# One-core decoder trunk: token factors spread by stride-zero transposes, and GpSimd normalising the probabilities of layer 0's second eight heads

## What is computed

```
def _rmsnorm(x, g):
    y = xf * lax.rsqrt(jnp.mean(xf * xf, axis=-1, keepdims=True) + EPS)
    return (y * g.astype(jnp.float32)).astype(x.dtype)

def _even_mixer(h, ...):            # layer 0
    proj = h @ w_in
    out_a = _blocked_causal_attn(...)      # 8 heads, forget-gate bias: heads 0 to 7 below
    out_b = _swa_with_sinks(...)           # 8 heads, window 128: heads 8 to 15 below
    return jnp.concatenate([out_a, out_b], axis=-1) @ w_out

# within _swa_with_sinks
    logits = jnp.where(mask, logits + bias, -jnp.inf)
    p = jax.nn.softmax(jnp.concatenate([logits, sink], axis=-1), axis=-1)[..., :-1]
    out = jnp.einsum("bnhgqk,bnkhd->bnqhgd", p.astype(v.dtype), vb)
```

## Time and profile before

| | us |
|---|---|
| time, median of 3 runs | 1150.34 |
| lowest and highest | 1149.0, 1150.37 |
| the profiled execution, its own time | 1150.78 |
| its span, first to last instruction | 1149.0 |
| PE busy in the span | 1114.7 |
| DVE, ACT, POOL busy | 878.7, 615.2, 388.0 |
| mean granted TensorE clock | 0.995 of 2.4 GHz |

### The profile page before, as it was taken

One profiled execution on the slowest core, in us unless ns is written; L12 is line 12 of the kernel. 1 busy time (PEld: TensorE's weight loads), 2 busy tenths in 40 slices (PEclk: granted clock), 3 DMA queues, 4 the chain that ended last, 5 costly groups with the idle time before them and its releaser, 6 DMA issues.

```text
span 1149.0 us, 16553 instructions
## 1 busy us (share of the span) xinstructions
PE 1114.7 (97%) x6033; PEld 944.6 (82%) x6037; DVE 878.7 (76%) x1485; ACT 615.2 (54%) x1094; POOL 388.0 (34%) x313
## 2 busy tenths in 40 slices
PE   7999999999999999999999999999999999999996
PEld 5788887888989989989967778888888888888885
DVE  6867787779668668768869999656778687787686
ACT  6777686554344354354475387854464443443443
POOL 2433433541140141151084365435521321311400
PEclk9999999999999999999999989999999999999999
DMA  5233341541522431431222000215322414315212
GB/s 167 76 115 100 103 121 42 165 129 47 174 74 72 148 89 57 146 91 55 83 74 65 28 2 27 65 38 160 116 73 92 146 56 152 99 41 183 73 37 91
DMA packets 142226, 105.55 MB, mean 92 GB/s; under 512 B 9078, under 2 KB 122017, under 8 KB 142162
## 3 DMA queue, kind: packets, MB, share of 16 engines
q1 hardware_dynamic: 140892, 104.61, 29.6%
q10 hardware_dynamic: 1270, 0.13, 0.1%
HBM read 102.56 MB, written 6.35 MB: 95 GB/s over the span
## 4 chain that ended last, share of the span: by engine, by line
PE 80%; DVE 11%; ACT 5%; issue 2%; DMA 1%; SPq 0%; ACTq 0%; DVEq 0%
PE bank L817 25%; PE bank L819 24%; PE bank L818 24%; ACT probs L1610 2%; DVE score L2552 2%; DVE probT_l L2076 1%; DVE best L2548 1%; PE bank L1027 1%; PE bank L1037 1%; PE bank L1038 1%; PE bank L1025 1%; DVE bank L2425 1%; DMA score<-in_x 1%; ACT wh L1359 1%; ACT ur L1359 1%
## 5 line engine op out<-in xcount | busy, mean ns | idle before, releaser
L1882 POOL TENSOR_TENSOR wl<-raw,wh 128x512 fp32r<-128x512 f32 x212 | 288.3, 1383 | 573.8 <-ACT wh L1359 549.9
L817 PE MATMUL bank<-ur,wh 128*128 128x512 f32 (+1 forms) x624 | 238.0, 381 | 0.2
L819 PE MATMUL bank<-ur,wl 128*128 128x512 f32 (+1 forms) x624 | 236.2, 378 | 0.0
L818 PE MATMUL bank<-ur,wh 128*128 128x512 f32 x560 | 218.0, 389 | 0.0
L1359 ACT ACTIVATE wh<-raw 128x1024 fp32r<-128x1024 f32 x107 | 111.9, 1053 | 120.4 <-PE bank L819 115.2
L817 PEld LDWEIGHTS bank<-ur,wh 128*128 128x128 f32 x624 | 117.4, 188 | 23.7 <-issue 2.5
L819 PEld LDWEIGHTS bank<-ur,wl 128*128 128x128 f32 x624 | 117.4, 188 | 21.9
L817 PE MATMUL bank<-ur 128*128 128x256 f32 (+3 forms) x352 | 119.0, 338 | 6.6 <-ACT probs L1610 2.6
L818 PE MATMUL bank<-xhl,wh 128*128 128x512 f32 (+1 forms) x336 | 124.2, 370 | 0.0
L818 PEld LDWEIGHTS bank<-ur,wh 128*128 128x128 f32 x560 | 105.2, 188 | 21.8 <-issue 0.5
L2258 DVE TENSOR_TENSOR xT<-bank,xT 128x512 f32<-128x512 f32 x112 | 74.5, 687 | 51.2 <-PE bank L819 51.1
(11 more groups left out here) (308 smaller groups left out, 2549.4 us busy)
## 6 DMA issues: line engine op xcount, KB each, us to landing
raw<-in_w_mlp SPq DMA_DIRECT2D x64, 512.0 KB, 4.0
raw<-in_w_in_e SPq DMA_DIRECT2D x18, 512.0 KB, 3.8
probs<-in_w_mlp SPq DMA_DIRECT2D x16, 512.0 KB, 4.4
rstd_qk<-in_w_mlp SPq DMA_DIRECT2D x16, 512.0 KB, 3.8
sq<-in_w_mlp SPq DMA_DIRECT2D x16, 512.0 KB, 4.8
raw<-in_w_in_o SPq DMA_DIRECT2D x10, 512.0 KB, 3.7
raw<-in_w_out_e SPq DMA_DIRECT2D x8, 512.0 KB, 3.8
score<-in_w_mlp SPq DMA_DIRECT2D x8, 512.0 KB, 6.2
```

Source lines behind the costliest of these rows:

```text
L817: mm(dst, lhs[0], rhs[0], start=start, stop=False, skip_group_check=not check)
L818: mm(dst, lhs[0], rhs[1], start=False, stop=False, skip_group_check=not check)
L819: return mm(dst, lhs[1], rhs[0], start=False, stop=stop, skip_group_check=not check)
L1882: return nc.gpsimd.tensor_tensor(dst, a, b, ALU.subtract)
```

## The change

It has two parts.

First, `diagonal` is gone. `spread` no longer multiplies ones by a diagonal matrix; it transposes, four times, a view of one column of `fin[:, 3, :]` that repeats it 128 times with stride zero. The semaphore that the diagonals raised (diag_ready) is replaced by factors_ready, which the last operation of `refined_root` raises.

Second, for heads 10 to 15 GpSimd runs `normalise`. VectorE's `sums(s + 1)` moves to the start of step s (9 to 14); its low halves of head s stand ahead of the maxima of head s+2. GpSimd's `normalise(s + 1)` stands at the head of its step s, and the spare slabs' splits no longer wait for probs_ready. Heads 8 and 9 are still normalised by VectorE.

```diff
             def spread(norm):
-                pe.wait_ge(diag_ready, NORMS.index(norm) + 1)
-                mm(bank[0][:, :], ones[:, :], sq[:, 0, :], start=True, stop=True).then_inc(spread_done, 1)
+                pe.wait_ge(factors_ready, NORMS.index(norm) + 1)
+                for a in range(NQ):
+                    last = nc.tensor.transpose(bank[0][:, P * a:P * (a + 1)], fin[:, 3, a:a + 1].to_broadcast([P, P]),
+                                               ident[:, :])
+                last.then_inc(spread_done, 1)
...
+            def normalise(j):
+                pool.wait_ge(rsum_ready, j + 1)
+                for blk, _, _, w, pc in units(j):
+                    pr = probs[:, j % 2, pc:pc + w]
+                    nc.gpsimd.tensor_scalar(pr, pr, rsum[:, j % 2, blk:blk + 1], None, ALU.mult).then_inc(probs_ready, 1)
...
             for s in FIRST_STEPS:
+                if NH < s < 2 * NH - 1:
+                    normalise(s + 1)
...
                 if s in SPARE_AT:
-                    pool.wait_ge(probs_ready, 4 * (s + 3))
                     split(SPARE_AT[s] % 2, SPARE_AT[s])
...
-            def diagonal(norm):
-                for a in range(NQ):
-                    last = v.tensor_scalar(sq[:, 0, P * a:P * (a + 1)], ident, fin[:, 3, a:a + 1], None, ALU.mult)
-                last.then_inc(diag_ready, 1)
...
+                if NH < s < 2 * NH - 1:
+                    sums(s + 1)
                 if 1 <= s:
                     outputs_summed(s - 1)
-                if NH <= s and s + 2 < 2 * NH:
-                    maxima(s + 2)
                 if 0 <= s:
                     probs_lo(s, (1,) if s < NH else range(2))
                 if NH <= s and s + 2 < 2 * NH:
-                    normalise(s + 2)
+                    maxima(s + 2)
```

More of the change, by code:

```diff
@@ L329, in trunk @@
         root_ready = sem("root_ready")
-        diag_ready = sem("diag_ready")
+        factors_ready = sem("factors_ready")
         spread_done = sem("spread_done")
@@ L1801, in _ @@
             root("mix_o")
-            act.wait_ge(diag_ready, NORMS.index("mix_o") + 1)
+            act.wait_ge(factors_ready, NORMS.index("mix_o") + 1)
             split_slab(N_IN1 + 2)
@@ L1831, in latent_values_hi @@
             def latent_values_hi(a):
-                act.wait_ge(diag_ready, NORMS.index("ckv") + 1)
+                act.wait_ge(factors_ready, NORMS.index("ckv") + 1)
                 act.wait_ge(dv_ready, a + 1)
@@ L2090, in refined_root @@
                 own.link(v.tensor_tensor(b, b, ms, ALU.mult))
-                own.link(v.scalar_tensor_tensor(fin[:, 3, cols], b, 1.5, y, ALU.add, ALU.mult))
+                v.scalar_tensor_tensor(fin[:, 3, cols], b, 1.5, y, ALU.add, ALU.mult).then_inc(factors_ready, 1)
+                dve.wait_ge(factors_ready, NORMS.index(norm) + stage + 1)
             def token_factors(norm):
@@ L2095, in token_factors @@
                 refined_root(norm)
-            def diagonal(norm):
-                for a in range(NQ):
-                    last = v.tensor_scalar(sq[:, 0, P * a:P * (a + 1)], ident, fin[:, 3, a:a + 1], None, ALU.mult)
-                last.then_inc(diag_ready, 1)
-            def spread_factors(norm):
-                token_factors(norm)
-                diagonal(norm)
             def take_factors(norm, dst, factor=None):
@@ L2116, in rsqrt @@
             def rsqrt(norm, dst):
-                spread_factors(norm)
+                token_factors(norm)
                 take_factors(norm, dst)
@@ L2578, in _ @@
             refined_root("mix_e")
-            diagonal("mix_e")
             v.memset(causal_strip[:, 0:S - P], 0.0)
@@ L2642, in _ @@
             take_slab(N_IN1 + 5)
-            spread_factors("cq")
+            token_factors("cq")
             top8()
@@ L2648, in _ @@
             top8()
-            spread_factors("ckv")
+            token_factors("ckv")
             top8()
```

## The result

The changed kernel takes **1154.61 us** (median of 5 runs, 1154.4 to 1155.98) where the kernel before takes 1149.28 on the same chip (5 runs, 1148.44 to 1150.37): a ratio of **1.0045**, 95% interval 1.0034 to 1.0056. It is slower by about 5 us. The forecast was 1149.1 with a range up to 1153.2, so the time lies outside it. The profiled execution took 1154.52 us around a span of 1152.7.

What follows compares the result with a forecast made beforehand. The prediction took TensorE, busy 97% of the span, as the bound. Spreads and diagonals gave -3.2 us, layer 0 +2.0, so 1150.34 - 1.2 = 1149.1 us, range 1146.4 to 1153.2.

Steps and rivals of the forecast that it cites:

- The spreads: Six spreads on TensorE: stride-zero transposes priced as ordinary ones, 0.42 us cheaper each, 2.5 us in all.
- VectorE's diagonals: Diagonals removed on VectorE: 0.64 us comes through in cq, 0.88 in ckv, of which 0.7 adds to the gain.
- The walk: In cq: the four transposes and their landing take some 0.67 us, after which take_factors can start.
- the list of signs: What would show the forecast: among others, cq's take_factors 1.3 us after the spread starts, with idle time ahead.
- VectorE's loop: Layer 0's steps on VectorE: 5.20 us before, 5.24 after, as low halves hand back the 1.1 us taken off.
- the wait for qb3: Layer 0, step 11: TensorE's 1.32 us wait for qb3's low halves goes, as these now lie under the exponentials.
- A head's price on GpSimd: Normalising one head on GpSimd: 1.8 us from the one-input row, bounds 1.34 and 2.7 (priced as two-input).
- The sum's term for layer 0: Loss in layer 0 from GpSimd's late normalises: 1.1 to 2.5 us, taken as 2.0.
- The queue: GpSimd in layer 0: normalises of heads 12 and 14 stand behind a slab's low half and output_lo, delaying TensorE's transposes.
- none before 11, 13, 15: Layer 0: TensorE waits 1 to 3 us for GpSimd's probabilities before heads 12 and 14, not before these odd heads.
- The clock: Rival: TensorE's clock halves in layer 0 after waits from about 2.6 us on, costing 3 us; 1152.6 us, chance 0.22.
- GpSimd is dear: Rival: GpSimd's normalise priced as two-input, layer 0 loses 5.2 us; 1152.3 us, chance 0.10.

Runs made afterwards that it cites:

- the probe: Separate kernel without the trunk, timing GpSimd's operations with VectorE idle or busy: the changed kernel's normalise form takes 921 ns for 256 columns with VectorE idle.
- two_op: The changed kernel with a second operation, add 0.0, in GpSimd's normalise: 1151.06 us, ratio 1.0006 to the kernel before.
- part2: The kernel before with only layer 0's part of the change, spreads by ones and diagonals kept: 1158.06 us, ratio 1.0078.
- old_order: The kernel before with transposed spreads, no diagonals; GpSimd multiplies heads 10 to 15 (add 0.0 behind) ahead of the spare slab; VectorE's order kept: 1146.14 us, ratio 0.9963.
- part1: The kernel before with only the transposed spreads and the diagonals gone, layer 0's heads as before: 1146.9 us, ratio 0.9974.
- order_alone: The changed kernel with normalise back on VectorE, and the spare slab's wait for probabilities restored: 1152.17 us, ratio 1.0023.

## Why the prediction was wrong, point by point

- **The spreads: right.** L868 takes 272 ns for each of 24 transposes; in mlp1 the second next matmul starts 0.67 us after the spread (821.09, 821.76), as said, where it was 1.09, and the third 0.90 (821.99) where it was 1.33 (817.68, 819.01): 0.43 less; 0.42 was said. Beside the ordinary transposes of the earlier trace rows, also 272 ns each and 0.67 us to the second next matmul, a stride of zero costs TensorE nothing that shows.

```profile
821.09 0.60 PE L868 MATMUL bank<-fixed,fin 128*128 128x128 f32 x4
821.45 0.48 PE L817 MATMUL bank<-ur,wh 128*128 128x512 f32 x1
821.76 0.39 PE L818 MATMUL bank<-ur,wh 128*128 128x512 f32 x1
821.99 0.40 PE L819 MATMUL bank<-ur,wl 128*128 128x512 f32 x1
```

- **VectorE's diagonals: half right.** Of cq the prediction said that only 0.64 of 3.03 us would come through, since `take_factors` waits for TensorE. It does, with 2.36 us of idle time ahead of it, 0.71 after the spread's start (623.54), and stands 6.0 us behind the old one where all around is 6.6 behind. (The walk had 0.67 for that distance and the list of signs 1.3, the distance before; the walk was right.) But the next operation gives the 0.6 back:

```profile
624.25 0.69 DVE L2115 TENSOR_TENSOR rstd_qk<-bank,rope 128x512 f32<-128x512 f32 x1 [2.36 <-PE bank L868]
624.98 1.69 DVE L2193 SCALAR_TENSOR_TENSOR ur<-tbuf,gain,ur 128x512 fp32r<-128x512 f32 x1
```

```profile
618.96 1.09 DVE L2190 SCALAR_TENSOR_TENSOR ur<-tbuf,gain,ur 128x512 fp32r<-128x512 f32 x1
```

The first is the change, the second before, behind the `take_factors` of the earlier trace rows. The operation takes 1.69 instead of 1.09 us. GpSimd splits a slab from 623.58 to 626.12 beside it, where before the split (616.97 to 619.52) ended halfway through it; that this overlap is the cause is argued from the two timelines and the probe, not shown by a run of its own. The 0.88 of ckv came through (0.8 by the landmarks). So part one is worth 0.4 for mix_e, 1.55 between the two row sums (before less two_op 582.67 - 581.13, and part2 less old_order 581.37 - 579.77, pairs with the same fall of the clock), and 0.4 for mlp1: 2.4 us, where 3.2 was said; the timing of part1, 3.0 (2.0 to 4.0), can't tell the two, and has whatever the clock gave in it.
- **VectorE's loop: right for the steps that were walked.** 5.24 us a step and no gain; order_alone shows it with the normalise on top, in three steps. And the wait for qb3 is gone in the change, as said.
- **A head's price on GpSimd: the step that failed.** "The one-input row is the nearer" took L1914, which has two operations, for L1990, which has one. 3.3 us was outside even the bound of 2.7, which came from two-input rows. The missing second operation was seen as less work, and it is more time. The sum's term for layer 0 was 2.0 us and measured 6.9; the price is 4.9 of these, as two_op shows.
- **The queue: right where it was walked.** Heads 12 and 14 were; head 10, which stands behind slab 20's low half and an `output_lo` in the same way, wasn't, though "none before 11, 13, 15" was right.
- **The clock: the rival came, its condition was wrong.** It was said to decide from a wait of about 2.6 us on, and the forecast left it out. Waits of 2.87 and 2.83 us were followed by half clock in the change and by a whole one in part2, and the 2.6 us wait for exponentials near 664, the same in all kernels, was followed by 6.8 us at half clock (before: PEclk 0.82 and 0.50 in 660 to 670), by 3.5 (part2: 0.81 and 0.84 in 670 to 680) or by none (part1, the change). The cost of that alone is read from the table's last column: 581.13 - 578.7 = 2.4 us for 6.8 us at half clock and 579.8 - 578.7 = 1.1 for 3.5. In layer 0 it makes up 3.9 of the 6.9 us, what the 3.0 us of added waits leave. (The 4.9 us of the form and these 3.9 are two cuts through the same loss: with the cheaper form waits and slow stretches both shrink; two_op has PEclk 0.84 in 175 to 180 and 0.82 in 180 to 185, 3.4 us at half clock.)
- **The sum, redone** for the profiled executions: 1150.78, less 2.4 for part one, 6.9 more in layer 0, 2.4 less for the clock near 665 us, 0.9 more at the start and 0.7 at the end are 1154.5, and 1154.52 was measured; the 0.9 and the 0.7 are read off, not explained. The forecast had neither of the clock's terms, which took each other's place in part: 3.9 in layer 0 against 2.4 near 665. Without the second, the profiled execution would have been further off. "GpSimd is dear" had the mechanism, at 5.2 us for a price of 2.7; I gave it 0.10, as I took the price for bounded.

## What to carry to other kernels

A price must come from a row of the same form: operations, operands and engine. Where there is none, the bounds from other forms are no bounds, and a small probe kernel gives the number. Work handed to a second engine pays only if the first engine's hidden work stays hidden and the second engine's whole period (here 10.6 us for two heads and 3.6 of waiting, against 12.1 for the two steps before) fits into the loop; reordering its queue, here, only changed who waited. And an experiment that undoes one thing should be read against its whole edit: order_alone brought back a wait as well.

## What the runs showed of the hardware

- GpSimd's `tensor_scalar` on float32 with one operation takes 924 ns for 256 columns, with a second that does nothing (add 0.0) 478. A copy of the same size took 398, a multiplication of two tensors 722. With a column as second operand, 554.
- Four transposes of a column repeated with stride zero cost what four ordinary ones cost, 272 ns each, and 0.67 us from the first to the second next matmul.
- Beside VectorE operations with two SBUF inputs, GpSimd's one-operation form on 256 columns went from 921 to 1433 ns, that with `add 0.0` from 478 to 711, its subtraction on 512 from 1262 to 1587.
- The same wait of 2.6 us was followed by no fall of TensorE's clock, by one of 3.5 us or by one of 6.8. Three kernels were profiled twice and each showed its own falls again, but the mean granted clock of one kernel's executions differs by up to 0.003 (part2, 0.991 to 0.994). What picks between them is open; the difference is worth up to 2.4 us here.
